# Hybrid decoder trunk on one core: value pages called forward, select steps with fewer small instructions, and part of B's level updates on GpSimd

## The chip, the cores and the metric

One core of one Trainium2 chip. The metric is the device time of one execution in microseconds, the median of several runs. Engines are named as the profile names them: PE (TensorE), PEld (its weight loads), DVE (VectorE), ACT (ScalarE), POOL (GpSimd), SP (SyncE, here only a DMA queue).

## The reference, cut to what matters

Two layers (DEPTH = 2) of a hybrid decoder run over 1024 prompt tokens and 8 x 4 sample tokens. A layer normalises, projects to four mixers A to D, mixes, and ends with a gated feed-forward part. What bears on the change:

```python
def mixer_a_sample(q, kv_new, iq, ik_new, iw, kv_pool, kidx_pool, page_table, bias_a):
    ...
    sc = indexer_scores(iq, iw, ik_all)
    sc = jnp.where(jnp.arange(L)[None, None, :] <= tpos[None, :, None], sc, NEG_BIG)
    val, idx = lax.top_k(sc, k_sel)              # k_sel = 256, for the prompt's rows as well
    ...
    return sparse_attend(q, kv_sel, tpos[None, :, None] - idx, val > 0.5 * NEG_BIG, bias_a)

def gla_chunk(s0, qc, kc, vc, lfc):              # mixer B, with a decay per token and channel
    bcum = jnp.cumsum(lfc, axis=2)
    diff = bcum[:, :, :, None, :] - bcum[:, :, None, :, :]
    decay = jnp.exp(jnp.where(causal[None, None, :, :, None], diff, NEG_BIG))
    att = jnp.einsum('nhtk,nhtsk,nhsk->nhts', qc, decay, kc)
    ...
```

Mixer A attends to the 256 keys with the highest indexer scores; keys and values of the sample group lie in pages of 128 tokens that a page table places. Mixer B (called B's retention levels in the change's words) is a gated linear attention.

## The kernel before, in words

Each engine has a program of its own; semaphores order them. The order of the projection stage is written out by hand in a table `STEPS_P` of 22 steps (lines 362 to 376): 3 for A, 6 and one for B (index `S_BI` = 9), 4 and one for C (`S_CV` = 14), 6 and one for D. A "T" step is three units of 24 matmuls of 352 columns, each with split weights (high and low parts); an "N" step is nine tiles of 24 matmuls. Before each step ScalarE writes the high part of the weights (`high_part`, two steps ahead) and GpSimd the low part (`low_weights`, line 532, two steps ahead: it waits for `wp_hi`).

Work on mixer A's sample group is hung between these steps on PE (`sample_a`, line 919). `SCORE_A` says behind which step the scores of which sequences stand, `MIX_A` (line 379) does so for the products with the values, `S_MASK`, `S_EXP`, `S_TURN` and `S_OUT` (line 380) for the mask product, the exponential, the turning of the probabilities through the diagonal `dgt`, and the output. Values lie in three buffers `KB`, for sequence n in number n % 3. Pages of values of sequences 1, 2, 4 and 6 are called by SP (lines 624 to 631), those of 0, 3, 5 and 7 by GpSimd: `CALLS` (line 381) gives the step at which GpSimd issues its 16 page transfers, after `low_weights(i + 2)` and after a wait for `as_v`, which counts sequences whose value product is done. At line 982 PE waits in front of step `S_B` for `ss_done` and `qz`.

Meanwhile VectorE runs `select()` (line 1946). It finds for every row the 256th largest score bit by bit: `thresholds` (line 1955) makes 32 passes, first for the sample group (one block of 32 x 2080), then for six prompt blocks of 128 x 384 to 1024. A pass builds a candidate from the threshold so far (line 1965), counts the scores that reach it (line 1960), turns the count into a bit (line 1969) and joins it (line 1971), each small instruction with a drain behind it. `chosen` then turns scores into a mask. Between passes of the prompt blocks `sample_softmax` (line 2007) takes the row maximum behind pass 4 (waits for the mask product, `as_qk`) and writes `dgt` behind pass 7 (waits for the exponential, `as_exp`); it waits for all values (`as_v`, line 2020) before the first prompt `chosen`. After `select()` VectorE joins `attend(0)`, the prompt's attention in mixer A: PE scores (line 820), VectorE adds the bias (line 2050), ScalarE takes the exponential. Each score block on PE waits for VectorE's add of the block before (`at_add`, line 816).

Mixer B follows (`gla(0)` on PE from line 1068, `gla_b` on VectorE from line 2205). Its 18 steps `STEPS_B` are 4 for the diagonal and, for levels 1 to 7, one for each r in 0 and 1. In a level step s, PE makes 32 matmuls of 64 columns (line 1129) into one of three bank pairs; VectorE waits for them (`g_att`), multiplies half of the queries `qf` (line 2235) and half of the keys `kg` (line 2236) by a block decay, counts that in `g_z`, and for s < 12 copies the products under a mask (line 2225); for the rest ScalarE evicts. PE's step (l, r) waits for the update of (l - 1, r), that is `g_z`, and for the copy of step s - 3 (`g_msk`). GpSimd has nothing to do in this part; its next work waits for `at_mix`.

Of the kernel before, what the change touches and what calls it, by code (L numbers as in the profile page):

```python
# [134 lines left out]
def build(nc, xT, wjobs, gains, consts, bits_u, ropet, decays, onehot, linemask, relb, lblog, ptab,  # L135
# [3 lines left out]
    with ctx:  # L139
# [69 lines left out]
        def sem(name):  # L209
# [32 lines left out]
            sem, ("g_qf", "g_z", "g_att", "g_msk", "g_msa", "g_sat"))  # L242
        g_ready, g_tr, g_kn, g_kv, g_s, g_in, g_vb = map(
# [53 lines left out]
        THR, CAND, KEEP, SGN = smu[:, 0:7], smu[:, 7:14], smu[:, 14:21], smu[:, 21:28]  # L297
        THRF, CANDF = THR.bitcast(F32), CAND.bitcast(F32)
# [73 lines left out]
        for r in range(6):  # L372
# [6 lines left out]
        MIX_A = {S_C + 3: (0, 1, 2), S_CV: (3, 4, 5), S_D + 1: (6, 7)}  # L379
        S_MASK, S_EXP, S_TURN, S_OUT = S_BI, S_C + 1, S_C + 2, S_D + 2  # L380
        CALLS = {S_B + 1: ("k", 3), S_B + 2: ("k", 5), S_B + 4: ("k", 7), S_BI: ("v", 0), S_C + 3: ("v", 3),
                 S_CV: ("v", 5), S_D + 1: ("v", 7)}
# [115 lines left out]
        def _(pool):  # L498
# [5 lines left out]
            with pool.Fori(0, DEPTH) as L:  # L504
# [41 lines left out]
                for i in range(NSTEP):  # L546
                    if i in CALLS:
                        call, n = CALLS[i]
                        places = page_numbers(pool, n)
                    if i + 2 < NSTEP:  # L550
                        low_weights(i + 2)
                    if i in CALLS:
                        (keys if call == "k" else values)(n, places)
                for j in range(J_OUT + NSLOT, NJOBS):
                    if j == J_OUT + NSLOT:
                        pool.wait_ge(at_mix, 2 * NU)
                        for k in range(2):
                            split_mix(k)
                    load(j, job_floats(j), j - NSLOT)
# [12 lines left out]
        def _(sp):  # L572
# [6 lines left out]
            with sp.Fori(0, DEPTH) as L:  # L579
# [98 lines left out]
                sp.wait_ge(g_z, 2)  # L678
                bias_tiles(1, 1)
# [48 lines left out]
        def _(pe):  # L728
# [190 lines left out]
            def sample_a(L):  # L919

                def scores(seqs):
                    for n in seqs:
                        if n in (3, 5, 7):
                            pe.wait_ge(kq_in[n], L * (32 * NPAGE) + 16 * NPAGE)
                        else:
                            pe.wait_ge(kp_in[n % 3], 16 * NPAGE * (1 + (n > 3)))
                    for b in range(5):
                        for n in seqs:
                            q = U[:, QZA + n * 32:QZA + n * 32 + 32]
                            o = KB[n % 3] + b * 512  # L930
                            k = U[:, o:o + 512] if b < 4 else aq[:, 2, SEQ:TT]
                            m = mm(PS[lane(n), b, 0:512 if b < 4 else NS], q, k, start=n < 4, stop=False,
                                   skip_group_check=True)
                            if b == 4:
                                m.then_inc(as_k, 1)
# [45 lines left out]
                for i in range(NSTEP):  # L981
                    if i == S_B:
                        pe.wait_ge(ss_done, 1)
                        pe.wait_ge(qz, 1)
                    if i == S_TURN + 1:
                        split_step(i, (0,))
                        pe.wait_ge(as_pt, 1)
                        turn(4)
                        split_step(i, (1, 2))
                        own_values()  # L990
                    else:
                        split_step(i)
                    if i in SCORE_A:
                        scores(SCORE_A[i])
                    if i in MIX_A:
                        values(MIX_A[i])
                    if i == S_MASK:
                        mask()
                    elif i == S_TURN:
                        pe.wait_ge(as_dg, 1)  # L1000
                        for b in range(4):
                            turn(b)
                    elif i == S_OUT + 1:
                        turn_out()
# [63 lines left out]
            def gla(k, steps):  # L1068
# [39 lines left out]
                for s, (l, r, half) in enumerate(steps):  # L1108
# [3 lines left out]
                    if l == 1:  # L1112
                        pe.wait_ge(g_qf, 1)
                    elif l >= 2:
                        pe.wait_ge(g_z, 2 * (l - 2) + r + 1)
                    if s >= 3 and s - 3 < NB_DVE:

                        pe.wait_ge(g_msk, NB_DVE * k + s - 2)
                    elif s >= 3:
                        pe.wait_ge(g_msa, s - 3 - NB_DVE + 1)  # L1120
# [19 lines left out]
                if k == 0:  # L1140
                    pe.wait_ge(g_z, 13)
                else:
# [10 lines left out]
                if k == 0:  # L1153
                    pe.wait_ge(g_z, 14)
                pe.wait_ge(g_kn, 3 * k + 1)
# [219 lines left out]
        def _(act):  # L1375
# [233 lines left out]
            def projections(L):  # L1609

                for i in range(NSTEP):
# [15 lines left out]
                    elif i == S_EXP - 1:  # L1627
                        table(ACT.Exp, 6)
                    elif i == S_EXP:
# [169 lines left out]
        def _(v):  # L1799
# [146 lines left out]
            def select():  # L1946
# [3 lines left out]
                v.memset(THR, 0)  # L1950
                v.memset(SGN, 1 << 31)
# [3 lines left out]
                def thresholds(blocks, c, between=lambda b: None):  # L1955

                    def counts(op, limit, into):
                        for s, m, i in blocks:
                            n = s.shape[1]
                            ts(U[0:m, JUNK[i]:JUNK[i] + n // 2].bitcast(BF16), s, limit[0:m, i:i + 1], None, op, ALU.add,  # L1960
# [3 lines left out]
                    def step(bit_u, bit_f):  # L1964
                        stt(out=CAND[:, c], in0=THR[:, c], scalar=bit_u, in1=SGN[:, c], op0=ALU.bitwise_or,
                            op1=ALU.bitwise_xor)
                        v.drain()
                        counts(ALU.is_ge, CANDF, CNT)
                        ts(KEEP[:, c], CNT[:, c], float(TOPK), bit_f, ALU.is_ge, ALU.mult)
                        v.drain()  # L1970
                        tt(out=THR[:, c], in0=THR[:, c], in1=KEEP[:, c], op=ALU.bitwise_or)
                        v.drain()

                    step(BITU[:, 0:1], cst(C_BITF, 1))

                    sgn = SGN[:, c].bitcast(I32)
                    ts(sgn, THR[:, c].bitcast(I32), 31, -1, ALU.arith_shift_right, ALU.bitwise_xor)
                    v.drain()
                    ts(sgn, sgn, -2 ** 31, None, ALU.bitwise_or)
                    v.drain()  # L1980
                    for b in range(1, 32):
                        step(BITU[:, b:b + 1], cst(C_BITF + b, 1))
                        between(b)
                    tt(out=THR[:, c], in0=THR[:, c], in1=SGN[:, c], op=ALU.bitwise_xor)
                    v.drain()
                    counts(ALU.is_gt, THRF, CGT)
# [5 lines left out]
                def chosen(s, m, i, half):  # L1992
# [3 lines left out]
                    ts(eq, s, THRF[0:m, i:i + 1], None, ALU.is_equal)  # L1996
# [5 lines left out]
                    stt(out=s, in0=s, scalar=THRF[0:m, i:i + 1], in1=cum, op0=ALU.is_gt, op1=ALU.add)  # L2002
# [4 lines left out]
                def sample_softmax(b):  # L2007
                    if b == 4:
# [4 lines left out]
                    elif b == 7:  # L2013
# [191 lines left out]
            def gla_b():  # L2205
# [24 lines left out]
                def update(l, r):  # L2230

                    w, n = 1 << (l - 1), TT if l < 3 else SEQ
                    qs, ks = (x[:, r, 0:n].rearrange("p (n s w) -> p n s w", s=2, w=w) for x in (qf, kg))
                    b = blk[l - 1][:, r, 0:n // w]
                    tt(out=qs[:, :, 1, :], in0=qs[:, :, 1, :], in1=bc(b[:, 0::2], 2, w), op=ALU.mult)
                    tt(out=ks[:, :, 0, :], in0=ks[:, :, 0, :], in1=bc(b[:, 1::2], 2, w), op=ALU.mult
# [362 lines left out]
```

## Time and profile before

| what | value |
|---|---|
| median of 3 runs (range) | 3400.09 us (3399.21 to 3400.72) |
| the profiled execution's own time | 3406.91 us |
| its span, first to last instruction | 3405.2 us |
| mean granted clock of PE in it | 0.949 of full speed |
| instructions | 56191 |

All durations below are of that one profiled execution. Times in a row are from the span's start. In a timeline row the first number is the start, the second the time taken (from the first instruction's start to the last one's end where several are merged), xN how many; in square brackets stands how long the engine was idle before and what released it. "issue" means that the engine waited for nothing that the profile shows. PEclk 1.00 is the full clock of 2.4 GHz, 0.50 is 1.2 GHz. A matmul in f32 counts more than once in xN.

### The profile page before, as it was taken

The numbers are of one execution on the slowest core, as the hardware profiler recorded it, in microseconds if no ns is written. First come the engines' busy times: TensorE is split into PE (matmuls) and PEld (weight loads), VectorE is DVE, ScalarE is ACT, GpSimd is POOL, SyncE is SP. The second block draws the span as 40 slices with busy tenths as digits, with TensorE's granted clock in tenths as the row PEclk, the third lists the DMA queues.
The fourth block names the chain that finished last, engine by engine and source line by source line (L and its number), as shares of the span: only waits on it lengthen the run. The fifth ranks groups of instructions, "written<-read, shape, count | busy, mean of one in ns | idle before, by whom it ended". The sixth has DMA issues, their size and how long they took to land.

```text
span 3405.2 us, 56191 instructions
## 1 busy us (share of the span) xinstructions
PE 3162.8 (93%) x21728; PEld 2887.3 (85%) x21728; DVE 1935.6 (57%) x3597; ACT 581.7 (17%) x1067; POOL 416.9 (12%) x594
## 2 busy tenths in 40 slices
PE   7999789898999999999999987898989999999997
PEld 5598786767899999999966987858678999999997
DVE  3699996678443333333426999966875333333335
ACT  3322113143210000000122221131432000000001
POOL 4133220001000000000041422200010000000000
PEclk9999889799999999999988998896999999999999
DMA  8144235132111111111141433252330111111112
GB/s 269 47 133 137 88 113 228 75 119 101 40 38 50 51 35 54 50 39 49 50 138 49 143 109 103 99 228 75 119 109 32 50 44 44 49 45 45 50 44 95
DMA packets 121149, 292.38 MB, mean 86 GB/s; under 512 B 19445, under 2 KB 70790, under 8 KB 116918
## 3 DMA queue, kind: packets, MB, share of 16 engines
q1 hardware_dynamic: 71938, 129.61, 11.0%
q0 software_dynamic: 33088, 102.84, 9.5%
q10 hardware_dynamic: 15844, 56.12, 4.7%
q8 instruction: 186, 3.05, 0.4%
q14 instruction: 93, 0.76, 0.1%
HBM read 242.24 MB, written 50.74 MB: 86 GB/s over the span
## 4 chain that ended last, share of the span: by engine, by line
PE 72%; DVE 17%; issue 7%; ACT 2%; DVEq 1%; POOL 1%; POOLq 1%; ACTq 0%; DMA 0%; SPq 0%
PE PS L1243 14%; PE PS L1241 14%; PE PS L1239 14%; DVE U L1960 7%; PE PS L896 3%; PE PS L759 3%; PE PS L1129 2%; PE PS L1265 2%; PE PS L1267 2%; PE PS L1266 2%; PE PS L781 2%; PE PS L820 2%; PE PS L910 2%; PE PS L859 1%; PE PS L840 1%
## 5 line engine op out<-in xcount | busy, mean ns | idle before, releaser
L1960 DVE TENSOR_SCALAR_CACHE_REDUCE U<-U,smu 32x2080 bf16<-32x2080 f32 (+6 forms) x462 | 504.8, 1146 | 13.9 <-issue 1.7
L2369 DVE TENSOR_TENSOR U<-PS,U 128x352 f32<-128x352 f32 x132 | 69.0, 523 | 546.3 <-ACT U L1751 546.2
L1243 PE MATMUL PS<-HNHR,WSR 128*128 128x352 f32 x1920 | 346.3, 322 | 0.0
L1239 PE MATMUL PS<-HNHR,WHR 128*128 128x352 f32 x1920 | 345.3, 321 | 0.0
L1241 PE MATMUL PS<-HnR,WHR 128*128 128x352 f32 x1920 | 345.3, 321 | 0.0
L1243 PEld LDWEIGHTS PS<-HNHR,WSR 128*128 128x128 f32 x1920 | 314.4, 188 | 0.0
L1239 PEld LDWEIGHTS PS<-HNHR,WHR 128*128 128x128 f32 x1920 | 313.5, 188 | 0.0
L1241 PEld LDWEIGHTS PS<-HnR,WHR 128*128 128x128 f32 x1920 | 313.5, 188 | 0.0
L507 POOL DMA_DIRECT2D WS<-wjobs x176 | 93.8, 533 | 1720.8 <-PE PS L1243 1472.7
L1751 ACT ACTIVATE U<-PS 128x352 f32<-128x352 f32 x132 | 61.3, 465 | 1347.8 <-PE PS L1243 1347.8
L1873 DVE CAST WHR<-WS 128x1024 fp32r<-128x1024 f32 (+2 forms) x152 | 94.4, 621 | 293.3 <-DMA WS<-wjobs 293.3
L1241 PE MATMUL PS<-HDLR,WHR 128*128 128x352 f32 x1056 | 200.7, 323 | 0.0
L1243 PE MATMUL PS<-HDHR,WSR 128*128 128x352 f32 x1056 | 200.6, 322 | 0.0
L1239 PE MATMUL PS<-HDHR,WHR 128*128 128x352 f32 x1056 | 200.5, 322 | 0.0
L537 POOL TENSOR_TENSOR WSR<-WS,HNHR 128x1024 fp32r<-128x1024 f32 x50 | 121.0, 2426 | 589.7 <-ACT HNHR L1377 589.7
L1243 PEld LDWEIGHTS PS<-HDHR,WSR 128*128 128x128 f32 x1056 | 175.2, 189 | 0.0
L1241 PEld LDWEIGHTS PS<-HDLR,WHR 128*128 128x128 f32 x1056 | 175.1, 188 | 0.0
L1239 PEld LDWEIGHTS PS<-HDHR,WHR 128*128 128x128 f32 x1056 | 174.8, 188 | 0.0
L896 PE MATMUL PS<-XHR,HNHR 128*128 128x352 f32 x912 | 168.4, 327 | 5.2 <-issue 5.2
L1875 DVE TENSOR_TENSOR WSR<-WS,WHR 128x1024 fp32r<-128x1024 f32 (+2 forms) x152 | 164.9, 1085 | 11.4
L896 PE MATMUL PS<-HnR,HNHR 128*128 128x352 f32 x912 | 165.8, 324 | 0.0
L896 PE MATMUL PS<-XHR,WSR 128*128 128x352 f32 x912 | 164.7, 322 | 0.0
(296 smaller groups left out, 5013.3 us busy)
## 6 DMA issues: line engine op xcount, KB each, us to landing
WS<-wjobs POOLq DMA_DIRECT2D x113, 512.0 KB, 3.9
WS<-wjobs ACTq DMA_DIRECT2D x50, 512.0 KB, 4.4
WS<-wjobs POOLq DMA_DIRECT2D x48, 384.0 KB, 3.4
Hn<-ckT SPq DMA_DIRECT2D x16, 896.0 KB, 10.8
U<-kT_pool SPq DMA_DIRECT2D x160, 64.0 KB, 2.1
xres<-U SPq DMA_DIRECT2D x2, 4224.0 KB, 15.4
U<-xres SPq DMA_DIRECT2D x4, 2112.0 KB, 8.3
U<-v_pool SPq DMA_DIRECT2D x128, 64.0 KB, 2.1
```

Of the source, the lines that this page charges most:

```text
L507: pool.dma_start(slot(j % NJOBS, n), wjobs[bass.ds(L * NJOBS + j, 1), :, 0:n].rearrange("a p n -> (a p) n")).then_inc(w_in[j % NJOBS % NSL ...
L537: pool.tensor_tensor(out=WSR[:, j % NSLOT, 0:1024], in0=slot(j, 1024), in1=high_weights(a).bitcast(F32), op=ALU.subtract).then_inc(wp_lo, 1)
L759: i = mm(PS[:, base + c, 0:CW], w[:, k, :], Hn[:, k, c * CW:(c + 1) * CW], start=k == 0, stop=k == KR - 1)
L781: m = mm(PS[:, b + o // 512, 0:w], iq[a:a + 64, r, i * P:(i + 1) * P], iq[a:a + 64, 2, o:o + w], start=True, stop=True)
L896: m = mm(out, w[:, k * P:(k + 1) * P], x[:, k, t], start=n == 0 and k == 0, stop=n == 2 and k == KR - 1)
L1239: mm(out, w(k)[0], x(k)[0], start=k == 0, stop=False)
L1241: mm(out, w(k)[0], x(k)[1], start=False, stop=False)
L1243: i = mm(out, w(k)[1], x(k)[0], start=False, stop=k == n - 1)
L1873: v.tensor_copy(hi, x)
L1875: return tt(out=lo, in0=x, in1=hi.bitcast(F32), op=ALU.subtract)
L1960: ts(U[0:m, JUNK[i]:JUNK[i] + n // 2].bitcast(BF16), s, limit[0:m, i:i + 1], None, op, ALU.add, accum_out=into[0:m, i:i + 1])
L2369: tt(out=x, in0=PS[:, 2 * (t % 3) + 1, 0:CW], in1=U[:, SIL + (t % 3) * CW:SIL + (t % 3 + 1) * CW], op=ALU.mult)
```

## The change

Four things change. (1) On GpSimd `CALLS` may hold several calls for one step: values of sequences 3 and 5 are called together at step 12, those of 7 at step 15. (2) The exponential and the turning stand one step earlier on ScalarE and PE (turning behind step 11 instead of 12), the value products behind 12, 15 and 17 instead of 13, 14 and 16, the output one step later; the row maximum is taken behind pass 2 instead of 4 and `dgt` written behind pass 5 instead of 7; PE's wait for `ss_done` and `qz` stands in front of the first scores instead of in front of step `S_B`. (3) A pass of `thresholds` keeps one candidate register `CAND`: instead of keep, join and build there are two instructions, `missed` (the bit's value where the count is too low) and one that combines that, the next bit and the candidate. (4) The key halves of the level updates are GpSimd's, counted in a new semaphore `g_zk`, for which PE and once SP wait beside `g_z`.

```diff
-        THR, CAND, KEEP, SGN = smu[:, 0:7], smu[:, 7:14], smu[:, 14:21], smu[:, 21:28]
+        CAND, MISS = smu[:, 0:7], smu[:, 7:14]
...
-        MIX_A = {S_C + 3: (0, 1, 2), S_CV: (3, 4, 5), S_D + 1: (6, 7)}
-        S_MASK, S_EXP, S_TURN, S_OUT = S_BI, S_C + 1, S_C + 2, S_D + 2
-        CALLS = {S_B + 1: ("k", 3), S_B + 2: ("k", 5), S_B + 4: ("k", 7), S_BI: ("v", 0), S_C + 3: ("v", 3),
-                 S_CV: ("v", 5), S_D + 1: ("v", 7)}
+        MIX_A = {S_C + 2: (0, 1, 2), S_D: (3, 4, 5), S_D + 2: (6, 7)}
+        S_MASK, S_EXP, S_TURN, S_OUT = S_BI, S_C, S_C + 1, S_D + 3
+        CALLS = {S_B + 1: (("k", 3),), S_B + 2: (("k", 5),), S_B + 4: (("k", 7),), S_BI: (("v", 0),),
+                 S_C + 2: (("v", 3), ("v", 5)), S_D: (("v", 7),)}
...
                 for i in range(NSTEP):
-                    if i in CALLS:
-                        call, n = CALLS[i]
-                        places = page_numbers(pool, n)
+                    calls = CALLS[i] if i in CALLS else ()
+                    numbers = [page_numbers(pool, n) for _, n in calls]
                     if i + 2 < NSTEP:
                         low_weights(i + 2)
-                    if i in CALLS:
+                    for (call, n), places in zip(calls, numbers):
                         (keys if call == "k" else values)(n, places)
+                for s, (l, r, _) in enumerate(STEPS_B):
+                    if l == 0:
+                        continue
+                    if r == 0:
+                        pool.drain()
+                    pool.wait_ge(g_att, s + 1)
+                    w, n = 1 << (l - 1), TT if l < 3 else SEQ
+                    ks = kg[:, r, 0:n].rearrange("p (n s w) -> p n s w", s=2, w=w)
+                    b = blk[l - 1][:, r, 0:n // w]
+                    pool.tensor_tensor(out=ks[:, :, 0, :], in0=ks[:, :, 0, :], in1=bc(b[:, 1::2], 2, w), op=ALU.mult
+                                       ).then_inc(g_zk, 1)
...
                 sp.wait_ge(g_z, 2)
+                sp.wait_ge(g_zk, 2)
                 bias_tiles(1, 1)
...
                 def scores(seqs):
+                    if 0 in seqs:
+                        pe.wait_ge(ss_done, 1)
+                        pe.wait_ge(qz, 1)
...
                 for i in range(NSTEP):
-                    if i == S_B:
-                        pe.wait_ge(ss_done, 1)
-                        pe.wait_ge(qz, 1)
...
                     elif l >= 2:
                         pe.wait_ge(g_z, 2 * (l - 2) + r + 1)
+                        pe.wait_ge(g_zk, 2 * (l - 2) + r + 1)
...
                     pe.wait_ge(g_z, 13)
+                    pe.wait_ge(g_zk, 13)
...
                     pe.wait_ge(g_z, 14)
+                    pe.wait_ge(g_zk, 14)
...
-                    elif i == S_EXP - 1:
+                    elif i == S_EXP:
                         table(ACT.Exp, 6)
-                    elif i == S_EXP:
                         sample_exp()
...
-                    def step(bit_u, bit_f):
-                        stt(out=CAND[:, c], in0=THR[:, c], scalar=bit_u, in1=SGN[:, c], op0=ALU.bitwise_or,
-                            op1=ALU.bitwise_xor)
-                        v.drain()
-                        counts(ALU.is_ge, CANDF, CNT)
-                        ts(KEEP[:, c], CNT[:, c], float(TOPK), bit_f, ALU.is_ge, ALU.mult)
-                        v.drain()
-                        tt(out=THR[:, c], in0=THR[:, c], in1=KEEP[:, c], op=ALU.bitwise_or)
-                        v.drain()
-                    step(BITU[:, 0:1], cst(C_BITF, 1))
-                    sgn = SGN[:, c].bitcast(I32)
-                    ts(sgn, THR[:, c].bitcast(I32), 31, -1, ALU.arith_shift_right, ALU.bitwise_xor)
+                    def missed(b):
+                        counts(ALU.is_ge, CNT)
+                        stt(out=MISS[:, c], in0=CNT[:, c], scalar=float(TOPK), in1=bc(cst(C_BITF + b, 1), 1, n)[:, :, 0],
+                            op0=ALU.is_lt, op1=ALU.mult)
+                        v.drain()
+                    missed(0)
+                    ts(CAND[:, c].bitcast(I32), MISS[:, c].bitcast(I32), 31, None, ALU.arith_shift_right)
                     v.drain()
-                    ts(sgn, sgn, -2 ** 31, None, ALU.bitwise_or)
+                    tt(out=CAND[:, c], in0=CAND[:, c], in1=bc(BITU[:, 1:2], 1, n)[:, :, 0], op=ALU.bitwise_xor)
                     v.drain()
                     for b in range(1, 32):
-                        step(BITU[:, b:b + 1], cst(C_BITF + b, 1))
+                        missed(b)
+                        if b < 31:
+                            stt(out=CAND[:, c], in0=MISS[:, c], scalar=BITU[:, b + 1:b + 2], in1=CAND[:, c],
+                                op0=ALU.bitwise_xor, op1=ALU.bitwise_xor)
+                        else:
+                            tt(out=CAND[:, c], in0=MISS[:, c], in1=CAND[:, c], op=ALU.bitwise_xor)
+                        v.drain()
                         between(b)
-                    tt(out=THR[:, c], in0=THR[:, c], in1=SGN[:, c], op=ALU.bitwise_xor)
-                    v.drain()
-                    counts(ALU.is_gt, THRF, CGT)
+                    counts(ALU.is_gt, CGT)
...
-                    if b == 4:
+                    if b == 2:
                         v.wait_ge(as_qk, 1)
...
-                    elif b == 7:
+                    elif b == 5:
                         v.wait_ge(as_exp, 1)
...
-                    qs, ks = (x[:, r, 0:n].rearrange("p (n s w) -> p n s w", s=2, w=w) for x in (qf, kg))
+                    qs = qf[:, r, 0:n].rearrange("p (n s w) -> p n s w", s=2, w=w)
                     b = blk[l - 1][:, r, 0:n // w]
-                    tt(out=qs[:, :, 1, :], in0=qs[:, :, 1, :], in1=bc(b[:, 0::2], 2, w), op=ALU.mult)
-                    tt(out=ks[:, :, 0, :], in0=ks[:, :, 0, :], in1=bc(b[:, 1::2], 2, w), op=ALU.mult
+                    tt(out=qs[:, :, 1, :], in0=qs[:, :, 1, :], in1=bc(b[:, 0::2], 2, w), op=ALU.mult
                        ).then_inc(g_z, 1)
```

## Rows read from the trace of the kernel before

**Rows 1.** The page, busy time of the engines.
```profile
PE 3162.8 (93%) x21728; PEld 2887.3 (85%) x21728; DVE 1935.6 (57%) x3597; ACT 581.7 (17%) x1067; POOL 416.9 (12%) x594
```

**Rows 2.** TensorE's waits, both layers: total us, times, longest us.
```profile
PE PS L954 <- DMA U<-v_pool: 66.3, 4, 17.7
...
PE PS L940 <- DVE dgt L2090: 17.9, 2, 9.0
...
PE PS L896 <- issue: 5.2, 2, 2.6
```

**Rows 3.** Windows, layer one: length, busy PE, PEld, DVE, ACT, POOL; PEclk, DMA, GB/s.
```profile
149.00:531.20 382.20, 336.82 (x2418) 323.94 (x2418) 356.41 (x709) 68.92 (x119) 113.65 (x135) 0.94 0.35 111
...
636.00:645.50 9.50, 7.21 (x125) 6.69 (x122) 8.77 (x10) 0.00 (x0) 0.00 (x0) 0.93 0.56 213
...
653.70:681.20 27.50, 27.50 (x257) 27.38 (x257) 14.75 (x20) 6.36 (x13) 0.00 (x0) 0.50 0.01 1
```

**Rows 4.** Timeline of PE and of DVE at the projections' end: start, us, instruction.
```profile
530.54 0.49 PE L820 MATMUL PS<-U 64*128 64x128 f32 x4 [0.47 <-ACT U L1377]
...
531.19 0.55 DVE L2029 MEMSET U<- 128x256 f32 x2 [0.16 <-issue]
...
531.67 0.28 DVE L2050 CUSTOM_DVE_ANT_0 U<-PS,U 128x128 f32<-128x128 f32 x1
```

**Rows 5.** Lines of POOL from 149 to 531 us; timelines of POOL and DVE.
```profile
L537 POOL TENSOR_TENSOR WSR<-WS,HNHR 128x1024 fp32r<-128x1024 f32 x23 | 54.7, 2382 | 253.1 <-ACT HNHR L1377 253.1
...
323.86 2.41 POOL L537 TENSOR_TENSOR WSR<-WS,HNHR 128x1024 fp32r<-128x1024 f32 x1 [9.01 <-ACT HNHR L1377]
...
397.61 8.53 POOL L492 DMA_DIRECT2D U<-v_pool  x16
...
324.00 2.30 DVE L1971 TENSOR_TENSOR smu<-smu 128x6 uint32<-128x6 uint32 x1
```

**Rows 6.** The chain in order of time: two T steps, one N step.
```profile
458.05 23.24 PE PS L896 x144
...
504.54 25.54 PE PS L910 x216
```

**Rows 7.** Timelines of PE (diagonal, mask) and of DVE (first prompt pass).
```profile
341.69 6.49 PE L940 MATMUL PS<-dgt,U 128*128 128x128 f32 x32 [8.97 <-DVE dgt L2090]
...
294.13 3.84 PE L964 MATMUL PS<-U,CT 48*128 48x512 f32 x10
...
281.76 0.21 DVE L1965 SCALAR_TENSOR_TENSOR smu<-smu,BITU 128x6 uint32<-128x6 uint32 x1
```

**Rows 8.** Timeline of DVE between two counts of the sample group.
```profile
158.26 0.21 DVE L1969 TENSOR_SCALAR smu<-sm,CT 128x1 uint32<-128x1 f32 x1
158.54 0.16 DVE L1971 TENSOR_TENSOR smu<-smu 128x1 uint32<-128x1 uint32 x1
158.78 0.22 DVE L1965 SCALAR_TENSOR_TENSOR smu<-smu,BITU 128x1 uint32<-128x1 uint32 x1
159.09 2.37 DVE L1960 TENSOR_SCALAR_CACHE_REDUCE U<-U,smu 32x2080 bf16<-32x2080 f32 x1
```

**Rows 9.** Lines of DVE by shape, 148 to 535 us.
```profile
L1971 DVE TENSOR_TENSOR smu<-smu 128x1 uint32<-128x1 uint32 x32 | 11.9, 372 | 2.4
```

**Rows 10.** Timelines of DVE and PE in B's levels.
```profile
640.36 0.75 DVE L2235 TENSOR_TENSOR U<-U 128x528 f32<-128x528 f32 x1
641.02 0.71 DVE L2236 TENSOR_TENSOR U<-U 128x528 f32<-128x528 f32 x1
641.63 2.44 DVE L2225 COPY_PREDICATED U<-CT,PS 128x1024 f32<-128x1024 int32 x1
...
641.78 2.00 PE L1129 MATMUL PS<-U 64*128 64x64 f32 x32 [0.73 <-DVE U L2236]
...
645.54 7.17 PE L1129 MATMUL PS<-U 64*128 64x64 f32 x64 [1.60 <-DVE U L2236]
...
653.67 27.57 PE L1129 MATMUL PS<-U 64*128 64x64 f32 x256 [0.95 <-DVE U L2236]
```

More of the change, by code:

```diff
@@ L242, in build @@
             sem, ("g_qf", "g_z", "g_att", "g_msk", "g_msa", "g_sat"))
+        g_zk = sem("g_zk")
         g_ready, g_tr, g_kn, g_kv, g_s, g_in, g_vb = map(
@@ L296, in build @@
         WSEL = sm[:, 96:128]
-        THR, CAND, KEEP, SGN = smu[:, 0:7], smu[:, 7:14], smu[:, 14:21], smu[:, 21:28]
-        THRF, CANDF = THR.bitcast(F32), CAND.bitcast(F32)
+        CAND, MISS = smu[:, 0:7], smu[:, 7:14]
+        CANDF = CAND.bitcast(F32)
         NRM = ((nrm_sq, nrm_acc, nrm_sum, nrm_inv), (first_sq, first_acc, first_sum, first_inv),
@@ L1949, in select @@
                 blocks = [(scs[i], P, i) for i in range(6)] + [(ss, NS, 6)]
-                v.memset(THR, 0)
-                v.memset(SGN, 1 << 31)
+                v.memset(CAND, 0)
                 v.memset(CGT, 0.0)
@@ L1955, in thresholds, with counts @@
                 def thresholds(blocks, c, between=lambda b: None):
-                    def counts(op, limit, into):
+                    n = c.stop - c.start
+                    def counts(op, into):
                         for s, m, i in blocks:
-                            n = s.shape[1]
-                            ts(U[0:m, JUNK[i]:JUNK[i] + n // 2].bitcast(BF16), s, limit[0:m, i:i + 1], None, op, ALU.add,
+                            w = s.shape[1]
+                            ts(U[0:m, JUNK[i]:JUNK[i] + w // 2].bitcast(BF16), s, CANDF[0:m, i:i + 1], None, op, ALU.add,
@@ L1995, in chosen @@
                     cum = U[0:m, FLAGS + half:FLAGS + half + n]
-                    ts(eq, s, THRF[0:m, i:i + 1], None, ALU.is_equal)
+                    ts(eq, s, CANDF[0:m, i:i + 1], None, ALU.is_equal)
                     v.drain()
@@ L2001, in chosen @@
                     v.drain()
-                    stt(out=s, in0=s, scalar=THRF[0:m, i:i + 1], in1=cum, op0=ALU.is_gt, op1=ALU.add)
+                    stt(out=s, in0=s, scalar=CANDF[0:m, i:i + 1], in1=cum, op0=ALU.is_gt, op1=ALU.add)
                     v.drain()
```

## The prediction

> **What bounds the kernel now.** The page comes first: TensorE is busy for 93% of the span [rows 1], so only stretches in which it waits or runs at half clock can give much back. The list of its waits names three that this change touches, each once or twice in each of the two layers [rows 2]: 66.3 us for pages of values, 17.9 us for the diagonal `dgt`, 5.2 us where only the sequencer shows ("issue") in front of the first projection behind `S_B`. Together they are 89.4 us, 44.7 us a layer, all in the projection stage of mixer A. It is tempting to predict that sum, and it would be wrong. The windows say why: from 149.0 to 531.2 us TensorE is busy for 336.8 of 382.2 us, VectorE for 356.4 [rows 3], and the rest of VectorE's time is gaps of 0.1 us between small instructions. The timeline of that stage's end shows the two engines arriving together: TensorE issues its first attention scores at 530.54, VectorE leaves `select()` with its memset at 531.19 and takes them at 531.67 [rows 4]. So the stage has two chains of the same length. VectorE's has nothing to wait for; TensorE's has 44.7 us of waits that end just in time. Taking time from TensorE's alone moves the end by nothing; the end moves by what VectorE's chain loses.
>
> **The change, part by part (one layer; layer two repeats it).**
>
> *Value pages called forward, turn one step earlier, later mixes one step later.* GpSimd now issues the pages for sequences 3 and 5 together, behind the first mix; before, the 16 calls of one sequence (8.53 us of issue, beginning at 397.61) stood behind the low weights of two steps on, and TensorE waited 17.7 us for them [rows 5, 2]. A pair of T steps takes 23.24 us and an N step 25.54 [rows 6]. Behind the two calls there now come two T steps and an N step before their use, 49 us; behind sequence 7's two T steps. The 17 and 8.5 us of issue fit. The 33.2 us of waits a layer go. The wait for `dgt` (9.0 us, ending at 341.69 [rows 7]) goes or shrinks to 1 or 2 us, since two passes fewer stand in front of it; the wait of 2.6 us is behind score work and goes. What is late next: VectorE. TensorE would be through near 531 - 45 - 8 (my estimate for the half rate behind each gap) = 478 us and wait there about 40 us for VectorE. Value of this part at the end: 0. What queues behind the moved calls on GpSimd is `low_weights` of the step after, at most 17 us later and needed behind an N step; SP's two calls keep their places and are released earlier with `as_v`. With VectorE's cover gone this part would be worth all 45 to 53 us.
>
> *Shorter select steps.* Between two counts stand three small instructions: keep, 0.28 us to the next start (158.26 to 158.54), or, 0.24 (to 158.78), candidate, 0.31 (to 159.09, where the next count starts) [rows 8]. With the count's 2.37 and its accumulator a pass takes 3.29. Per `thresholds()` the small work is 32 x (0.31 + 0.28 + 0.24) + 3 single ones (two for the sign, one last xor) x 0.24 = 27.3 us. After: 32 `missed` at 0.28 to 0.31 (a three-operand form, so I take 0.30), 30 candidates at 0.31, 3 single at 0.24 = 19.7 us. That is 7.6 us less, for the sample group and again for the prompt blocks: **-15.2 us a layer**, every one on VectorE's chain. Bounds: `missed` at 0.28 gives -16.6; at 0.40 (no small one shown is as slow unblocked) -9.0.
>
> *What VectorE may wait for newly.* The row maximum moves from behind pass 4 to behind pass 2 of the prompt blocks and needs the mask product, which ends at 294.13 + 3.84 = 297.97 [rows 7]. TensorE gets there 4.2 us earlier (the 2.6 us wait and, an estimate, 1.6 us at half rate behind it): 293.8. The prompt passes began at 281.76 [rows 7]; less 7.6 they begin at 274.2, and three passes of 6.0 end at 292.2. Wait 1.6, or more or less by where a GpSimd multiplication falls: **+2.0** (0 to 3). The exponential's maximum is then there at 296.7 and its result near 311, before pass 5 ends at 315: no wait. The last values are there near 416, before `chosen` at about 487: no wait.
>
> *Stalls of VectorE by GpSimd.* At 324.00 an or of 128x6 that takes 0.17 us elsewhere took 2.30 us; GpSimd's subtraction ran from 323.86 for 2.41 us and both ended together [rows 5]. Means show the sum: the 128x1 or takes 372 ns over 32 of them [rows 9], where an unblocked one takes 160 [rows 8]: 0.212 x 32 = 6.8 us a layer in the sample passes alone. The 23 subtractions stay 23 [rows 5], so the stalls stay too, on other instructions: **0** (-3 to +3). The Trainium skill has it as an exclusive lock ("SBUF — State Buffer", "SBUF: two separate sides"): an instruction of VectorE with two SBUF inputs and one of GpSimd never run together. The row agrees.
>
> *Start of attention.* Scores for the first block now lie ready, 0.5 us less; TensorE restarts after a long idle time. It ran at half clock there before too, so **0** (-0.5 to +3).
>
> *Key side on GpSimd (B's levels).* VectorE's update is 0.66 us of query and 0.61 of key (640.36 to 641.02 to 641.63), then 2.4 us of predicated copy; TensorE's 32 matmuls of a level step wait for it at 641.78 and 645.54 [rows 10]. That is a period of 3.5 us for the first four steps. From 653.67 eight steps run for 27.57 us without a gap, 3.45 each, at granted clock 0.50 (1.2 GHz) [rows 10, 3]: there TensorE is the bound and VectorE's 0.61 is worth nothing. Five key halves (steps 4 to 8) stand in front of 653.67, so overlap alone would give 5 x 0.62 = 3.1 us. GpSimd has no such multiplication in the trace; nearest is 2.38 us for 1024 contiguous elements [rows 5], so 1.2 for 512, up to 2.4 if strides cost double. By the stall row the query and key halves exclude each other when both are released by the same matmul: if GpSimd comes first at step 4, VectorE loses 1.2 once, and the gain is 1.9. By the Trainium skill's lock this term lies between those two ends, without one it is the larger. I take **-2.6**. Behind them, the last key half is due when TensorE has done `values(0)`, 4 us after its release: covered. The waits `g_zk` on SP delay only a bias tile for the second attention. Bounds: -13 (first rival below), +3 (clock falls already at step 4).
>
> Sum: -15.2 + 2.0 + 0 + 0 - 2.6 = **-15.8 us a layer, -31.6 in all**. The profiled execution took 3406.91 us (span 3405.2), so 3375.3 by its own time; the median of the runs shown is 3400.09, 0.2% lower, so 3368.5.
>
> **The rivals.**
> 1. *The levels stay at full clock.* At 636 to 645.5 the granted clock was 0.93, with gaps before 641.78 and 645.54, and 0.50 afterwards [rows 3, 10]. Smaller gaps might keep 2.4 GHz; then ten steps run near 2.1 instead of 3.4 us: 11 to 13 us a layer more, 3345. Against it: 27.5 us of unbroken matmuls of this kind at 1.2 GHz did not lift the clock. The Trainium skill's rule, that activity releases the throttle ("TensorE: Matmul & The Clock Gate", "Part 1: The HAM clock gate"), speaks for this rival; by the trace alone continuous work was not enough here. 0.13.
> 2. *All of TensorE's waits come back*: 3400 - 2 x 53 - 5 = 3289. It needs VectorE to have slack before 531.19, and it has none. 0.03.
> 3. *No change*: `missed` with its broadcast operand costs 0.5 or more, or new stalls eat the passes: 3395 to 3405. 0.05.
> 4. *Slower: GpSimd's multiplication becomes the bound of the levels.* Fourteen steps take 45 us now (636 to 681.2 [rows 3]), 3.2 each. If a key half takes x, the levels take 14x; above x = 4.2 us the 13.2 us won by select is gone, at 5 us the layer is 25 - 13 = 12 us longer: 3424. For it: strided and broadcast operands that the trace doesn't have on GpSimd. Against it: 1.2 us by size, 3.5 times too little. 0.04.
>
> **How the numbers follow.** My own case has 0.75 and spans 3358 to 3382: select between -16.6 and -12, the new wait 0 to 3, stalls 3 either way, levels 0 to -3. The predicted time is its value, 3368. Down to 3345 it takes in rival 1, up to 3383 the poor ends together; outside are rivals 2, 4 and most of 3. A measurement of this kernel can tell about 0.2% (7 us) from no change. Faster 0.75 + 0.13 + 0.03 = 0.91, same 0.05, slower 0.04.
>
> **What would show it.** Right: `thresholds` without the third small instruction, period near 3.05 and 6.0 us; no wait for `v_pool`; TensorE's largest new wait, about 40 us a layer, in front of the second score block of the first attention, released by VectorE; stage end near 518. Level steps with VectorE multiplications only on `qf`, period 2.9 us at first, 3.4 at half clock later. Wrong: attention starting before 505 or behind 525; a clock of 1.0 in the levels; GpSimd's halves over 3 us, or VectorE's query half stretched to 1.5 us at each step.

## The result and the profile after

The changed kernel takes 3365.26 us in the median (six runs, 3360.20 to 3382.13), the kernel before beside it 3399.65: ratio 0.990, 95% interval 0.987 to 0.993. That is 34 us; 3368.0 had been predicted. The profiled execution took 3366.62 us.

Page of the changed kernel, span and busy time (before: [rows 1]).
```profile
span 3364.9 us, 55933 instructions
...
PE 3146.4 (94%) x21728; PEld 2873.4 (85%) x21728; DVE 1903.3 (57%) x3431; ACT 582.2 (17%) x1067; POOL 463.2 (14%) x622
```
Its waits of TensorE: total us, times, longest us (before: [rows 2]).
```profile
PE PS L832 <- DVE sm L2063: 75.5, 8, 36.0
```
The waits for pages and for the diagonal are gone (0.5 us is left of the latter) and have come back as one, 36.0 us a layer, for VectorE in front of the second block of scores. TensorE's timeline shows where its own chain ends (before: [rows 4]):
```profile
478.68 0.49 PE L832 MATMUL PS<-U 64*128 64x128 f32 x4 [0.47 <-ACT U L1392]
515.18 1.22 PE L832 MATMUL PS<-U 64*128 64x256 f32 x4 [36.01 <-DVE sm L2063]
```
The windows say the same: TensorE is busy for 328.7 of 364.5 us, VectorE for 344.6.

Windows of the changed kernel, layer one: the projection stage, B's levels from step 7 on, the end of the second attention (before: [rows 3]).
```profile
149.70:514.20 364.50, 328.74 (x2418) 316.09 (x2418) 344.57 (x640) 68.76 (x119) 114.47 (x135) 0.95 0.41 132
...
625.70:660.20 34.50, 34.48 (x321) 34.36 (x322) 16.97 (x22) 6.37 (x13) 13.34 (x9) 0.50 0.01 2
756.00:766.00 10.00, 8.55 (x90) 4.15 (x90) 9.74 (x11) 0.94 (x3) 7.14 (x4) 0.66 0.22 57
```
Timelines of the changed kernel: VectorE at the stage's end (before: [rows 4]), two small instructions of a sample pass and the next count (before: [rows 8]), and the row maximum.
```profile
514.15 0.55 DVE L2042 MEMSET U<- 128x256 f32 x2 [0.16 <-issue]
...
161.03 0.16 DVE L1981 SCALAR_TENSOR_TENSOR smu<-sm,CT 128x1 uint32<-128x1 f32 x1
161.26 0.22 DVE L1993 SCALAR_TENSOR_TENSOR smu<-smu,BITU 128x1 uint32<-128x1 uint32 x1
161.58 2.37 DVE L1975 TENSOR_SCALAR_CACHE_REDUCE U<-U,smu 32x2080 bf16<-32x2080 f32 x1
...
294.95 2.33 DVE L2023 TENSOR_REDUCE sm<-PS 128x1 f32<-128x2080 f32 x1
```

Where the time went, in stretches of layer one, measured from one instruction to the same one in each trace (in us; "stage" runs from the first count to the memset behind the last block, "attention" from there to B's first matmul, which is one of the diagonal, "levels" to the first matmul behind the last level step, "behind" from there to the out projection):

| kernel | stage | attention | levels | behind |
|---|---|---|---|---|
| before | 379.1 | 93.2 | 56.8 | 245.4 |
| after | 361.8 | 90.6 | 55.3 | 249.9 |
| select steps alone | 368.5 | 91.6 | 56.1 | 244.3 |
| calls alone | 380.4 | 91.4 | 55.4 | 244.0 |
| key side alone | 379.0 | 93.2 | 55.4 | 250.0 |
| after, no key side | 362.1 | 90.5 | 56.6 | 245.3 |
| after, 8 pieces | 354.0 | 91.4 | 55.4 | 249.9 |
| and row maximum later | 346.5 | 90.9 | 55.4 | 249.9 |

Before the first count the change also drops one small instruction, 0.3 us. So a layer wins 17.7 us in the stage, 2.6 in the attention and 1.4 in the levels, and gives 4.5 back behind them: 17.2, twice 34.4, the difference of the medians. The two profiled executions are 40.3 us apart: 7.2 us lie in the preparation of layer two's scores, which nothing in the change touches (last section).

### The profile page after: what moved, and what is told of

Same layout as the page of the kernel before. It is cut to its first block, busy times and chain, and to the rows that moved or that the text cites. A ratio compares the mean times of both kernels' runs of the same rounds, so it can differ in the third digit from the quotient of the medians.

```text
span 3364.9 us, 55933 instructions
## 1 busy us (share of the span) xinstructions
PE 3146.4 (94%) x21728; PEld 2873.4 (85%) x21728; DVE 1903.3 (57%) x3431; ACT 582.2 (17%) x1067; POOL 463.2 (14%) x622
## 4 chain that ended last, share of the span: by engine, by line
PE 67%; DVE 27%; issue 3%; ACT 2%; DVEq 1%; DMA 0%; ACTq 0%; SPq 0%; POOL 0%; POOLq 0%
DVE U L1975 15%; PE PS L1258 14%; PE PS L1256 14%; PE PS L1254 14%; PE PS L771 3%; PE PS L1142 3%; PE PS L1280 2%; PE PS L1282 2%; PE PS L1281 2%; PE PS L832 2%; DVE smu L1981 1%; DVE smu L1993 1%; PE PS L852 1%; PE PS L793 1%; PE PS L871 1%
```

## Experiments

**The parts one by one.** The calls are the hunks on the schedule and the row maximum, the select steps the hunk in `thresholds`, the key side `g_zk` and the loop on GpSimd; each was put alone into the kernel before.

> The kernel before with the shorter select steps alone. My theory: mixer A's stage has two chains of one length, and both must be shortened. VectorE's loses about 17 us a layer (as in the changed kernel), but TensorE's keeps its waits for value pages; of its waits only the one for dgt can shrink, by up to 8 us a layer. So the stage gains 0 to 8 us a layer: 3384 to 3400 us, the likeliest 3390, and VectorE waits 9 us or more for TensorE's first attention scores. The rival, that the select steps alone give what the changed kernel gained in that stage: 3365 us.

Measured: 3374.76 us against 3393.67 before on its chip, ratio 0.994 (0.991 to 0.996): 19 us by the medians, 21 by the ratio. Faster than the 3384 to 3400 that I gave my theory, slower than the rival's 3365. Its waits of TensorE:
```profile
PE PS L954 <- DMA U<-v_pool: 66.0, 4, 17.5
...
PE PS L896 <- issue: 5.2, 2, 2.6
...
PE PS L940 <- DVE dgt L2089: 0.5, 1, 0.5
```
The waits for pages stand as before, that for the diagonal (9.0 us a layer) went whole, and stage and attention together lost 12 us a layer (472.3 to 460.1). TensorE's chain, from the first count to its first attention scores, fell from 378.5 to 368.1 us. In layer two VectorE was through at 360.6 and waited 7.1 us for TensorE's scores: here TensorE ends the stage.

> The kernel before with the value pages called forward, the turn a step earlier and the mixes later, alone (row maximum behind pass 2). My theory: TensorE's waits of 45 us a layer go and come back in one piece in front of the first attention, since VectorE's chain is untouched: 3400 us, 3392 to 3406 with what the clock does, stage end at 531 as before. The rival, that removed waits are won: 3310 us or less.

Measured: 3398.00 us against 3393.67, ratio 1.000 (0.998 to 1.002). Its waits:
```profile
PE PS L819 <- DVE sm L2048: 92.1, 8, 44.4
PE PS L942 <- DVE dgt L2088: 17.4, 2, 8.7
```
33 us a layer of waits for pages were turned into one of 44.4 us, and the stage ended at 532.7. The wait for the diagonal stayed at 8.7 us: it goes by the select steps, not by the earlier turn. TensorE's chain took 336.6 us here, 326.3 in the changed kernel. A wait that disappears from the list without moving the end: this is what reading the second chain guards against.

> The changed kernel with the value pages called as before, the turn and mixes at their old steps and the row maximum behind pass 4. My theory: TensorE's waits are back and bound the stage, so it gives back all but 0 to 8 us a layer: 3381 to 3397 us, the select steps' gain mostly lost. The rival, that forwarding the calls is worth nothing: 3365 us.

```diff
-MIX_A = {S_C + 2: (0, 1, 2), S_D: (3, 4, 5), S_D + 2: (6, 7)}
+MIX_A = {S_C + 3: (0, 1, 2), S_CV: (3, 4, 5), S_D + 1: (6, 7)}
```
(and `CALLS`, `S_EXP`, `S_TURN`, `S_OUT`, PE's wait for `ss_done` and the row maximum with it). Measured: 3376.83 us, ratio 0.993 (0.991 to 0.995), like the select steps alone and a little better than I gave it. So the calls are worth 0 alone and about 12 us (0.990 against 0.993) once VectorE's chain is shorter; the select steps 21 alone and about 33 with the calls (0.990 against 1.000). The intervals of 0.990 and 0.993 overlap; the traces bear the 12 us out: both layers together, from the first count to the out projection, took 13.4 us more without the calls.

> The changed kernel with 24 instead of 32 bits in the threshold of the prompt blocks; the eight lowest bits of those thresholds are left out. It takes 8 passes of 5.93 us, 47 us, from VectorE's chain and nothing from TensorE's. My theory: TensorE, which is through its stage 36 us before VectorE's end, becomes the bound: the stage ends about 36 us earlier, the wait of 36 us shrinks to under 2: 3293 us. The rival, that TensorE's end moves with VectorE's (the softmax passes feed it, then the pages): the whole 47 us a layer or less than 25: 3271 us, or over 3315 us.

```diff
-                    for b in range(1, 32):
+                    last = 31 if n == 1 else 23
+                    for b in range(1, last + 1):
...
-                        if b < 31:
+                        if b < last:
```
Measured: 3297.90 us, ratio 0.969 (0.967 to 0.972). Stage and attention took 418.4 us where the changed kernel took 452.4: of the 47 us cut, 34 were won. The wait of 36 us is gone. TensorE is still in its last projection when VectorE is through, and now VectorE waits:
```profile
481.40 0.55 DVE L2043 MEMSET U<- 128x256 f32 x2 [0.16 <-issue]
...
491.67 0.49 PE L832 MATMUL PS<-U 64*128 64x128 f32 x4 [0.47 <-ACT U L1392]
...
492.33 0.29 DVE L2064 CUSTOM_DVE_ANT_0 U<-PS,U 128x128 f32<-128x128 f32 x1 [10.37 <-PE PS L832]
```
In this execution the stage began 13.0 us later than in the changed kernel's (its first count at 165.41 against 152.40; last section). From the first count to TensorE's first scores it is 326.3 us in both kernels, in both layers: TensorE's end did not move with VectorE's, so the rival is out, and this chain is the next bound.

**The key side.**

> The kernel before with the key side of B's levels on GpSimd, alone. From the changed kernel's levels (55.4 us against 56.8) 1.4 us a layer: 3397 us; the clock of the stages behind may move it by 5 us either way. The rival, that GpSimd's share costs VectorE what it saves: 3400 us and query halves stretched beyond 1 us at most steps.

> The changed kernel with the key side back on VectorE. My theory: the select steps and the calls carry nearly all of it: 3368 us (1.4 us a layer more than the changed kernel). The rival, that the key side carries a good part, as predicted at 2.6 us a layer or more: 3370 to 3375 us.

Measured: alone 3404.19 us, ratio 1.003 (1.001 to 1.004), slower, outside my 3397 and also the rival's 3400, which placed the cost in the levels; without it, 3356.94 us on a chip where the kernel before took 3393.67, ratio 0.990 (0.987 to 0.993), the changed kernel's own: by its time the key side can't be seen there, the interval is 9 us to either side. The traces see it, and both agree on where: levels 1.3 us shorter, everything behind them 4.6 longer (table). What lies there is GpSimd's split of the first halves of mixer B's result. GpSimd in the kernel before, and with the key side alone; then VectorE's eight rotary and decay multiplications in both:
```profile
780.50 1.06 POOL L527 CAST HDLR<-U 128x1056 fp32r<-128x1056 f32 x1 [279.10 <-DVE U L2073]
790.96 2.42 POOL L529 TENSOR_TENSOR HNHR<-U,HDLR 128x1056 fp32r<-128x1056 f32 x1 [9.40 <-issue]
...
780.88 5.58 DVE L2308 TENSOR_TENSOR Hn<-Hn,CT 128x1024 f32<-128x1024 f32 x8 [0.45 <-issue]
```
```profile
778.30 1.06 POOL L528 CAST HDLR<-U 128x1056 fp32r<-128x1056 f32 x1 [96.71 <-DVE U L2089]
779.51 3.23 POOL L530 TENSOR_TENSOR HNHR<-U,HDLR 128x1056 fp32r<-128x1056 f32 x1
...
778.33 11.30 DVE L2323 TENSOR_TENSOR Hn<-Hn,CT 128x1024 f32<-128x1024 f32 x8
```
Before, 9.40 us of "issue" stood between GpSimd's cast and its subtraction, and VectorE's multiplications ran undisturbed in 5.58 us. With the key side in front the gap is gone; both subtractions fall on the multiplications and stretch them to 11.30 us, and TensorE waits 3.5 us for them. The multiplications are stretched so in every trace: 11.3 us in all sixteen layers with the key side on GpSimd and the split at its place, 5.6 to 5.9 in the eight without.

> The changed kernel, with GpSimd waiting for the end of VectorE's decay masks in front of the split of mixer B's first halves. In all traces with the key side on GpSimd these two subtractions start 1.2 us behind the cast; in the others they start 10.5 us behind it. My theory: in the early place they stretch VectorE's rotary and decay multiplications, which bound that stretch, and this is what the key side costs: the stretch from the end of the levels to the out projection loses 4.5 us a layer against the kernel before and gets back 3 to 5 of them: 6 to 10 us under the changed kernel. The rival, that the loss is TensorE's clock, which stands at half speed at another place: no difference, within 4 us.

```diff
                         pool.wait_ge(at_mix, 2 * NU)
+                        pool.wait_ge(g_sat, 2)
```
Measured: 3361.44 us, ratio 0.991 (0.989 to 0.993), beside 3364.90 and 0.991 (0.989 to 0.993) for the changed kernel on the same chip: my 6 to 10 us are not there. The trace shows why. VectorE's multiplications are whole again, but TensorE ran the 48 matmuls beside them at half clock, and the subtractions now stretch the VectorE work of the sample states; TensorE waits for that instead:
```profile
756.51 5.04 DVE L2321 TENSOR_TENSOR Hn<-Hn,CT 128x1024 f32<-128x1024 f32 x8
...
757.48 4.95 PE L1069 MATMUL PS<-U 128*32 128x256 f32 x48
...
785.38 1.97 PE L1201 MATMUL PS<-Hn,U 64*64 64x128 f32 x16 [4.22 <-DVE U L2166]
```
The same two in the changed kernel without the key side:
```profile
760.77 2.80 PE L1055 MATMUL PS<-U 128*32 128x256 f32 x48
...
784.61 2.61 PE L1184 MATMUL PS<-Hn,U 64*64 64x128 f32 x22 [2.32 <-DVE U L2149]
```
So in the late place the loss has two other terms: 2.15 us of clock (4.95 against 2.80) and 1.9 us of wait (4.22 against 2.32). In the early place the clock is no term of it. The 48 matmuls and TensorE's wait for the multiplications, with the key side alone and in the changed kernel:
```profile
778.85 2.80 PE L1069 MATMUL PS<-U 128*32 128x256 f32 x48
790.81 1.85 PE L1143 MATMUL PS<-Hn 64*128 64x128 f32 x16 [3.54 <-DVE U L2335]
...
759.57 5.14 PE L1068 MATMUL PS<-U 128*32 128x256 f32 x48
771.08 2.02 PE L1142 MATMUL PS<-Hn 64*128 64x128 f32 x16 [0.75 <-DVE U L2332]
```
What the slow clock took, the wait gave back, and the stretch behind the levels is 250.0 and 249.9 us long: VectorE bounds it either way. My theory named the loss rightly, but not what stood behind it. What the late place would give at full clock isn't shown; all four layers with it ran these matmuls at half clock. Why the clock falls there is open: they took 4.9 to 5.1 us in 14 of 20 layers with the key side and in 1 of 8 without.

**The stalls of VectorE.**

> The changed kernel with each of GpSimd's subtractions of 1024 columns cut into four of 256. VectorE's instructions lose about 22 us a layer by being stretched to the end of a subtraction (2.4 us each), and VectorE bounds the stage with TensorE waiting 36 us for it. My theory, that a VectorE instruction waits only for the GpSimd instruction in flight: the stretches fall to 4 to 9 us a layer, the stage ends 13 to 18 us earlier: 3330 to 3342 us. The rival, that both share a port and slow each other by the elements that GpSimd has to move however they are cut: 3365 us, or a little more.

> The same, cut into eight of 128 columns. My theory: stretches of 0.3 us at most, 3 to 6 us a layer, 3327 to 3338 us, a little under the four pieces, unless a fixed cost of each GpSimd instruction makes the subtractions together much longer than 2.4 us. The rival: 3365 us or more.

```diff
-pool.tensor_tensor(out=WSR[:, j % NSLOT, 0:1024], ...).then_inc(wp_lo, 1)
+for c in range(0, 1024, 128):
+    m = pool.tensor_tensor(out=WSR[:, j % NSLOT, c:c + 128], ...)
+m.then_inc(wp_lo, 1)
```
Measured: 3355.57 us, ratio 0.987 (0.984 to 0.989), and 3353.05, 0.986 (0.984 to 0.988), the kernel before at 3401.72 on that chip. By the ratios that is 11 and 13 us under the changed kernel's 0.990, less than half of what I expected; the intervals just overlap with the changed kernel's, but the stage shrank in both layers of both traces, from 361.8 to 356.2 and 354. The stretches did fall, and by more than the rival of a shared port allows: the small instructions of the sample passes, changed kernel and then eight pieces (busy us, mean ns):
```profile
L1981 DVE SCALAR_TENSOR_TENSOR smu<-sm,CT 128x1 uint32<-128x1 f32 x32 | 12.1, 378 | 2.4
L1993 DVE SCALAR_TENSOR_TENSOR smu<-smu,BITU 128x1 uint32<-128x1 uint32 x30 | 10.6, 355 | 2.6 <-issue 0.5
```
```profile
L1983 DVE SCALAR_TENSOR_TENSOR smu<-sm,CT 128x1 uint32<-128x1 f32 x32 | 8.6, 268 | 2.4
L1995 DVE SCALAR_TENSOR_TENSOR smu<-smu,BITU 128x1 uint32<-128x1 uint32 x30 | 7.6, 252 | 2.6 <-issue 0.5
...
293.95 2.33 DVE L2025 TENSOR_REDUCE sm<-PS 128x1 f32<-128x2080 f32 x1 [7.75 <-PE PS L981]
```
Unstretched they take 160 and 220 ns. The last line is where the rest went: VectorE now reaches the row maximum 7.75 us before TensorE has the mask product. This is the wait that the prediction put at 2.0 us for the changed kernel, where it is nothing.

> The changed kernel once more, unchanged, on the chip of the three runs beside it, so that they can be compared with it: 3357 to 3370 us, ratio to the kernel before 0.990.

> The changed kernel with GpSimd's subtractions in eight pieces and the row maximum back behind pass 4 (the row normalisation behind pass 7). With pieces alone VectorE came early enough to wait 6.5 to 7.8 us for the mask product in front of the row maximum. My theory: two passes later nothing is waited for, the prompt passes take 195 us instead of 202.4 and the stage ends 7 to 8 us earlier a layer: 14 to 16 us under the kernel with eight pieces alone, 3337 to 3342 us. The rival, that the wait comes back elsewhere (the exponential, the turn or TensorE's values late by two passes): no more than 5 us under it.

> The same with the later split of mixer B's halves as well. If both theories hold the two gains add: 6 to 10 us under it, 3328 to 3336 us. If the loss behind the levels is the clock's: the same as without, 3337 to 3342 us.

```diff
-                    if b == 2:
+                    if b == 4:
                         v.wait_ge(as_qk, 1)
```
(the row normalisation from 5 to 7 with it). Measured on one chip, the kernel before at 3391.79: the changed kernel again 3364.90; pieces and later row maximum 3329.96, ratio 0.981 (0.979 to 0.983); with the later split 3330.42, 0.980 (0.978 to 0.982). The stage shrank by 7.4 us in layer one and 8.8 in layer two, where 7 to 8 were expected; the time is 7 us better than my 3337 to 3342. With the later split the time lies where I had put it if both gains add, but so does the time without it: the split adds nothing that can be told. The kernel with eight pieces and the row maximum behind pass 4 beats both: 62 us under the kernel before, 35 under the changed one.

## Why the prediction was right, point by point

- **VectorE's chain sets the end, TensorE's waits are worth nothing by themselves.** Right: the calls alone gave 1.000, and TensorE waits 36.0 us where "about 40 us" stood. Its projections, put to end near 478, end there (first scores at 478.68), and its chain is 52.2 us shorter, of the 45 to 53 reckoned. But not all of it is this part's: of the two waits, the one for the diagonal was to go because two passes fewer stand in front of it, and with the calls alone it stayed at 8.7 us. And "value of this part at the end: 0" holds only for the calls alone. With the select steps in place the calls are worth 12 of the 34 us, since without them TensorE's chain ends the stage. The step that failed is the bookkeeping by parts: with two chains of one length the gain belongs to the pair.
- **Shorter select steps, -15.2 us a layer.** Too small. A pass lost 0.29 us (sample) and 0.31 (prompt), where 0.22 was reckoned: `missed` takes 0.23 to the next start, not 0.30 (0.16 busy, where the form that it replaced took 0.21). Without stretches that is 20 us.
- **Stalls, 0.** Wrong in sign, inside its 3 us. Summed as what each instruction took over the shortest of its form, the stretches grew in the sample passes from 6.8 to 11.0 us, in the whole stage from 19.4 to 21.9. In seven overlaps of the sample passes before, the first small instruction behind a count, which reads one tensor, was never stretched, only the second, which reads two. The new first one reads two and was stretched in five overlaps. But the form isn't the whole cause. The calls alone, with the old instructions, have 11.1 us in the sample passes too: GpSimd's subtractions come up to 4.5 us earlier there, ten of them in these passes instead of nine, and fall on other instructions. In the prompt passes the old first instruction, over 128x6, was stretched as well, in five of six.
- **The mask, +2.0.** 0 here (the row maximum starts at 294.95, the mask was through at 294.24): the sample passes had lost 4.2 us to the stretches and VectorE came later. With the pieces it came early and waited 7.75. The mechanism was right and its place too; its size hung on the term before it.
- **Start of attention, 0.** It gave 2.6 us a layer, outside the bounds. Two things were misread. ScalarE was left out: before, it was still issuing weight transfers when VectorE took the first scores, and its first exponential of them came 3.1 us later (534.76 against 531.67); now these transfers are issued while TensorE waits for VectorE, and it comes 1.1 us later (515.70 against 514.63). TensorE, which waited 2.4 us for it at 535.3, no longer waits. And the restart wasn't at half clock before: the second block's scores took 0.70 us then and 1.22 now, 0.5 us that the term should have had.
- **Key side, -2.6.** The levels gave 1.4. TensorE's clock falls at the same step as before, 21 us behind B's first matmul (625.72 here, 645.54 then), and the ten steps from there are its own: 3.4 us each without a gap. Of the steps in front little was won, because VectorE's query halves took 1.32 and 1.77 us beside GpSimd's key halves, where 0.75 is the undisturbed time [rows 10]; the waits of 0.73, 1.60 and 0.95 us [rows 10] became two of 0.17 and 2.03. Five steps at 0.62 was too many, and one stretch too few. The larger failure is that the price was looked for in the levels alone. Behind them it cost 4.5, by GpSimd's split coming 9.4 us earlier. Net it costs 3 us a layer. The sum had -5.2 for both layers and needed +6.
- **Rival 1, full clock in the levels.** It didn't come: 34.5 us of unbroken matmuls, clock 0.50. The Trainium skill ("TensorE: Matmul & The Clock Gate", "Part 1: The HAM clock gate") has sustained activity release the clock; this window contradicts it as [rows 3] did. Rival 4: a key half took 1.15 to 2.1 us, far from 4.2.
- The total was right partly because misses cancelled: select -4.6, the mask -2.0 and attention -2.6 against stalls +2.5, the key side and what follows it +5.7 a layer; -15.8 predicted, -17.2 measured (0.4 us is in none of them).

## What to carry to other kernels

When two engines reach the end of a stage together, price the pair of edits and each alone, and say which chain each shortens; a list of waits shows neither. When work moves to an engine that shares access with another, follow that engine's queue beyond the stretch: what stands behind the moved work now starts at another time, and its new neighbour pays. If a small instruction has to wait for a long one, cutting the long one into pieces is cheap and, once the waits that it uncovers are moved too, was worth 35 us here, as much as the whole change.

## What the runs showed of the hardware

VectorE's small instructions waited for the end of GpSimd's subtraction in flight. In the changed kernel:
```profile
163.24 2.41 POOL L538 TENSOR_TENSOR WSR<-WS,HNHR 128x1024 fp32r<-128x1024 f32 x1 [29.43 <-ACT HNHR L1392]
...
164.02 1.64 DVE L1981 SCALAR_TENSOR_TENSOR smu<-sm,CT 128x1 uint32<-128x1 f32 x1
```
They end at 165.65 and 165.66. The count, which reads one operand and accumulates, ran beside subtractions in all seven overlaps of the sample group at its 2.37 us. That is what the Trainium skill says of an exclusive lock held for a whole instruction ("SBUF — State Buffer", "SBUF: two separate sides"), and the pieces bear it out: less held at a time, less stretch, though GpSimd's own 23 subtractions grew from 55 to 81 us.

GpSimd's first subtraction behind 279 us of idle time stood 9.40 us of "issue" behind its cast, the same in the changed kernel without the key side (311 us idle), and 0.15 us or less where multiplications had run 97 to 111 us earlier. What the gap is no row says.

TensorE's clock changes the length of stretches that have nothing to do with an edit. The same 20 matmuls of the score preparation in layer one and layer two of one execution of the kernel before:
```profile
105.19 7.23 PE L781 MATMUL PS<-U 64*128 64x512 f32 x20 [0.49 <-ACT U L1515]
...
1793.88 11.23 PE L781 MATMUL PS<-U 64*128 64x512 f32 x20 [1.11 <-ACT U L1515]
...
1780.00:1800.00 20.00, 17.77 (x31) 8.85 (x31) 13.30 (x15) 7.94 (x11) 0.00 (x0) 0.50 0.01 2
```
Over all 28 such preparations (two layers of fourteen traces) 20 took 121.3 to 122.9 us, four 128.7 to 129.2, one 131.9 and three 136.0 to 136.4. One of the last was in the profiled execution of the kernel before, which took 7 us more than the median; no trace of a median execution is there to compare. Another was in layer one of the run with 24 bits. A difference of up to 15 us between two single executions of this kernel is no evidence before this stretch has been looked at in both.
